# The pooling stage of a two-layer decoder step: other queues, other engines and other PSUM banks for its parts

## The reference, cut to what matters

```
cs = concat([zeros, cumsum(x_ext, axis=1)])
for g, w in enumerate((2, 4, 8, 16)):            # 256 channels each
    lo   = max(i + 1 - w, 0);  cnt = i + 1 - lo
    mean = (cs[i + 1] - cs[lo]) / cnt            # mean of the last w tokens
    d_g  = mean - x
out = einsum('btgc,gce->btge', d, w_pool) * pool_scale
x   = layernorm(ALPHA * x + out)
```

## Time and profile before

| | |
|---|---|
| median of 3 runs | 2095.04 us (2094.93 to 2096.57) |
| the profiled execution's own time | 2099.22 us |
| its span, first to last instruction | 2097.4 us |
| granted TensorE clock, mean | 0.965 |
| PE busy | 1963.5 us (94%) |
| DVE, ACT, POOL busy | 839.8, 589.9, 500.9 us |

### The profile page before, as it was taken

One profiled execution on the slowest core, in us unless ns is written; L12 is line 12 of the kernel. 1 busy time (PEld: TensorE's weight loads), 2 busy tenths in 40 slices (PEclk: granted clock), 3 DMA queues, 4 the chain that ended last, 5 costly groups with the idle time before them and its releaser, 6 DMA issues.

```text
span 2097.4 us, 36040 instructions
## 1 busy us (share of the span) xinstructions
PE 1963.5 (94%) x15430; PEld 1882.6 (90%) x15430; DVE 839.8 (40%) x1133; ACT 589.9 (28%) x822; POOL 500.9 (24%) x439
## 2 busy tenths in 40 slices
PE   7999999999988769999999999999996599999996
PEld 7999999987955558999999999999996499999996
DVE  3333322446867315333332253333225553333223
ACT  3122221333244414322122151212125352121123
POOL 3211112241310525211112131111112631111120
PEclk9999999999989879999999999999998799999998
DMA  6443222361100222223322323332221223323321
GB/s 201 145 151 100 82 89 96 87 151 41 44 1 1 84 78 81 81 81 99 90 85 91 96 81 85 95 95 85 91 91 39 62 69 92 98 82 95 97 71 41
DMA packets 260094, 179.59 MB, mean 86 GB/s; under 512 B 10870, under 2 KB 257022, under 8 KB 259485
## 3 DMA queue, kind: packets, MB, share of 16 engines
q1 hardware_dynamic: 250000, 154.90, 25.3%
q10 hardware_dynamic: 7893, 10.83, 1.9%
q0 software_dynamic: 2112, 12.59, 1.7%
HBM read 169.62 MB, written 8.08 MB: 85 GB/s over the span
## 4 chain that ended last, share of the span: by engine, by line
PE 84%; issue 6%; DVE 4%; POOL 3%; ACT 2%; DMA 1%; ACTq 0%; POOLq 0%; DVEq 0%
PE ps L845 72%; PE ps L866 3%; PE ps L972 3%; PE ps L915 2%; PE ps L977 1%; DVE w_lo L1336 1%; ACT w_hi L539 1%; PE ps L956 1%; POOL sum_sq L1873 1%; PE ps L1051 1%; POOL k_sel L1939 1%; POOL sum_z L1871 1%; PE ps L1220 1%; POOL diag L1951 1%; PE ps L994 0%
## 5 line engine op out<-in xcount | busy, mean ns | idle before, releaser
L845 PE MATMUL ps<-xh,w_hi 128*128 128x260 f32 x2880 | 592.2, 284 | 21.1 <-DVE w_lo L1336 17.4
L1336 DVE TENSOR_TENSOR w_lo<-w_raw,w_hi 128x2048 fp32r<-128x2048 f32 (+2 forms) x153 | 445.8, 2914 | 392.2 <-ACT w_hi L539 392.2
L845 PE MATMUL ps<-xh,w_lo 128*128 128x260 f32 x2880 | 589.0, 283 | 0.0
L845 PEld LDWEIGHTS ps<-xh,w_hi 128*128 128x128 f32 x2880 | 453.1, 190 | 22.8 <-DVE w_lo L1336 12.1
L845 PEld LDWEIGHTS ps<-xh,w_lo 128*128 128x128 f32 x2880 | 453.2, 190 | 0.1
L845 PE MATMUL ps<-xl,w_hi 128*128 128x260 f32 x2880 | 362.7, 283 | 0.0
L539 ACT CAST w_hi<-w_raw 128x2048 fp32r<-128x2048 f32 (+2 forms) x153 | 282.0, 1844 | 271.1 <-PE ps L845 264.0
L845 PEld LDWEIGHTS ps<-xl,w_hi 128*128 128x128 f32 x2880 | 352.9, 189 | 0.0
L845 PE MATMUL ps<-hh,w_hi 128*128 128x260 f32 x1408 | 292.9, 283 | 0.0
L845 PE MATMUL ps<-hh,w_lo 128*128 128x260 f32 x1408 | 291.4, 282 | 0.0
L1802 DVE TENSOR_TENSOR hid<-silu_g,ps 128x520 f32<-128x520 f32 x88 | 61.3, 696 | 553.6 <-ACT silu_g L755 531.7
(11 more groups left out here) (257 smaller groups left out, 1670.2 us busy)
## 6 DMA issues: line engine op xcount, KB each, us to landing
w_raw<-in_ffn_wi_dram SPq DMA_DIRECT2D x176, 512.0 KB
w_raw<-in_ffn_wo_dram SPq DMA_DIRECT2D x32, 1024.0 KB
w_raw<-in_ffn_wo_dram SPq DMA_DIRECT2D x16, 768.0 KB
w_raw<-in_attn_w_in_dram SPq DMA_DIRECT2D x8, 1024.0 KB
keys_scratch<-key_half POOLq DMA_DIRECT2D x2, 2048.0 KB, 7.9
w_raw<-in_attn_w_o_dram SPq DMA_DIRECT2D x4, 1024.0 KB
x_in<-in_x_prompt_dram ACTq DMA_DIRECT2D x4, 512.0 KB, 10.0
out_dram<-y_out ACTq DMA_DIRECT2D x4, 512.0 KB
```

What stands on the lines that cost most here:

```text
L845: mm = nc.tensor.matmul(ps[0:mc, bank + 2 * m + h, 0:HT], w[:, k, m, 0:mc], x(k)[:, h * HT:(h + 1) * HT], start=first and k == 0 and w is ...
L1336: nc.vector.tensor_tensor(w_lo[:, c % 2, 0:n], w_raw[:, c % 2, 0:n], w_hi[:, c % 2, 0:n].bitcast(F32), ALU.subtract).then_inc(s_lo, 1)
```

## The change

Everything concerns the pooling stage and its neighbours:

- **Weights**: one chunk of 1 MB for all four groups; the stage has 1 chunk where it had 4. The `f2` tail now splits this chunk and the first chunk of `f3`.
- **Values once**: `affine` writes `xf` alone. The first window addition reads `xf` and writes `win[1]`; GpSimd copies column 0.
- **State**: GpSimd issues both state transfers once `f2`'s last product is done. ACT evicts the transposed state (`state_columns`) between the two halves of the `f2` tail, ahead of `root(st, 1)`.
- **Last rows**: prompt and decode rows in one set of 8 transposes (were 16), two evictions (were four), in `last_rows`, behind the rounding of group 1.
- **Group 3's windows** remain with GpSimd and start with its own first addition of `xf`.
- **Order**: DVE makes `pooled(g)` and then `mixed(g - 1)`, the residual addition of the group before, as four instructions of 260 columns. All groups use banks 0, 2, 4, 6, so a group's products wait for the residual additions of the group before.
- **Means**: `sums` is gone in this stage. `tile_stats` multiplies each tile of x and of its square by the matrix of 1/1024 into banks 1, 3, 5, 7, between the groups' products; 32 matmuls where there were 24. ACT's squares wait for `s_sqd`, which TensorE raises per tile.

The diff, cut to its core:

```diff
@@ -512,11 +518,10 @@
     def poolmix(name):
         st = plan[name]
-        for g in range(4):
-            c = st.chunk + g
-            sp.wait_ge(s_lo, c + 1)
-            sp.dma_start(w_raw[:, c % 2, 0:512].rearrange("p (k c) -> p k c", k=2),
-                         a["pool_w"][0, g].rearrange("(k p) c -> p k c", p=P)).then_inc(s_raw[c % 2], 32)
+        c = st.chunk
+        sp.wait_ge(s_lo, c + 1)
+        sp.dma_start(w_raw[:, c % 2, :].rearrange("p (k c) -> p k c", k=KD),
+                     a["pool_w"][0].rearrange("g (k p) c -> p (g k) c", p=P)).then_inc(s_raw[c % 2], 32)
     for name in plan:
         if name == "pr":
...
@@ -555,23 +563,14 @@
         act.wait_ge(s_rv, 2 * st.ln + h + 1)
         nc.scalar.activation(moment(1, h), moment(1, h), ACT.Sqrt).then_inc(s_rstd, 1)
-    def affine(n, st, h, split, order, windows, begin, end):
+    def affine(n, st, h, split, order, begin, end):
         for at_ in range(begin, end):
             d = order[at_]
             act.wait_ge(s_t, 2 * KD * st.ln + KD * h + at_ + 1)
-            if windows:
-                if h == 0 and at_ == 0:
-                    act.wait_ge(s_wpad, 1)
-                t0, t1 = (0, HT) if h == 0 else (HT, SEQ)
-                nc.scalar.activation(win[0][:, d, 16 + t0:16 + t1], xf[:, d, t0:t1], ACT.Identity, bias=offset(n, d),
-                                     scale=gain(n, d)).then_inc(s_win, 1)
-            elif split:
+            if split:
                 nc.scalar.activation(xh[:, d, cols(h)], xf[:, d, cols(h)], ACT.Identity, bias=offset(n, d),
                                      scale=gain(n, d)).then_inc(s_xh, 1)
-            if windows and h == 1:
-                nc.scalar.activation(xf[:, d, HT:SEQ], xf[:, d, HT:SEQ], ACT.Identity, bias=offset(n, d), scale=gain(n, d))
-            t = slice(SEQ, TOK) if windows and h == 1 else cols(h)
-            nc.scalar.activation(xf[:, d, t], xf[:, d, t], ACT.Identity, bias=offset(n, d),
+            nc.scalar.activation(xf[:, d, cols(h)], xf[:, d, cols(h)], ACT.Identity, bias=offset(n, d),
                                  scale=gain(n, d)).then_inc(s_xf, 1)
     def warm(func):
...
@@ -704,23 +706,24 @@
         root(st, 0)
         if nxt is not None:
             split_hi(nxt + 1)
-        ahead = 0 if windows else 2
-        affine(n, st, 0, split, order, windows, 0, ahead)
+        ahead = 2 if between is None else 0
+        affine(n, st, 0, split, order, 0, ahead)
         for d in range(KD - 2, KD):
             act.wait_ge(s_free, first_free + d + 1)
             nc.scalar.activation(sq[:, d % 2, cols(1)], xf[:, d, cols(1)], ACT.Square).then_inc(s_sq, 1)
-        affine(n, st, 0, split, order, windows, ahead, ahead + 3)
+        affine(n, st, 0, split, order, ahead, ahead + 3)
         moments(st, 1)
-        affine(n, st, 0, split, order, windows, ahead + 3, KD)
+        affine(n, st, 0, split, order, ahead + 3, KD)
+        if between is not None:
+            between()
         root(st, 1)
-        affine(n, st, 1, split, order, windows, 0, KD)
+        affine(n, st, 1, split, order, 0, KD)
     def mixer_out(name, n, nxt):
         st = plan[name]
         for g in range(4):
-            if g > 0 or name == "op":
-                split_hi(st.chunk + g + 1, 0, 512 if name == "pl" and g < 3 else CHUNK)
+            split_hi(st.chunk + g + 1)
             if g < 3:
                 squares(st, 4 + 2 * st.group, g)
         tail(n, st, 4 + 2 * st.group, nxt, True)
...
@@ -728,27 +731,33 @@
     def poolmix(name):
         st = plan[name]
-        act.dma_start(state_in[:], a["state_pool"].rearrange("l b r d -> (l b r) d")).then_inc(s_st_in, 16)
-        act.dma_start(outs[9][:, :, 0:PBUF - 1, :].rearrange("l b r d -> (l b) r d"),
-                      a["state_pool"][:, :, 1:PBUF, :].rearrange("l b r d -> (l b) r d")).then_inc(s_tailo, 16)
+        for g in range(4):
+            for d in (2 * g, 2 * g + 1):
+                act.wait_ge(s_diff, d + 1)
+                nc.scalar.activation(xh[:, d, :], diff[:, d, :], ACT.Copy).then_inc(s_xh, 1)
+            if g == 1:
+                last_rows()
+            if g >= 1:
+                squares(st, 4 + 2 * st.group, g - 1)
+        tail(4, st, 4 + 2 * st.group, plan["f3"].chunk, True)
+    def state_columns():
         for q in range(2):
             act.wait_ge(s_st, q + 1)
             nc.scalar.activation(state_t[:, 4 * q:4 * q + 4].rearrange("p d b r -> p d (b r)"),
                                  ps[:, 6 * q, :].rearrange("p (d n) -> p d n", d=4)[:, :, 0:DEC * PBUF],
                                  ACT.Copy).then_inc(s_ste, 1)
+    def last_rows():
         act.wait_ge(s_tail, 1)
-        for n, rows in enumerate((PBUF, DEC)):
-            for q in range(2):
-                nc.scalar.activation(tail_rows[0:rows, n, q * 512:(q + 1) * 512], ps[0:rows, 2 + 2 * n + q, :],
-                                     ACT.Copy).then_inc(s_taile, 1)
-        act.wait_ge(s_taile, 4)
-        act.dma_start(outs[5].rearrange("l b r d -> (l b r) d"), tail_rows[0:PBUF, 0, :]).then_inc(s_tailo, 16)
-        act.dma_start(outs[9][0, :, PBUF - 1, :], tail_rows[0:DEC, 1, :]).then_inc(s_tailo, 16)
-        for d in range(KD):
-            act.wait_ge(s_diff, d + 1)
-            nc.scalar.activation(xh[:, d, :], diff[:, d, :], ACT.Copy).then_inc(s_xh, 1)
-        mixer_out(name, 4, plan["f3"].chunk)
+        for q in range(2):
+            nc.scalar.activation(tail_rows[:, q * 512:(q + 1) * 512], ps[0:PBUF + DEC, 3 + 4 * q, :],
+                                 ACT.Copy).then_inc(s_taile, 1)
+        act.wait_ge(s_taile, 2)
+        act.dma_start(outs[5].rearrange("l b r d -> (l b r) d"), tail_rows[0:PBUF, :]).then_inc(s_tailo, 16)
+        act.dma_start(outs[9][0, :, PBUF - 1, :], tail_rows[PBUF:PBUF + DEC, :]).then_inc(s_tailo, 16)
     def gates(st, j, off):
         act.wait_ge(s_used, off + (2 + st.chunk + j + 1))
...
@@ -1265,16 +1268,69 @@
                                          state_in[:, (4 * q + d) * P:(4 * q + d + 1) * P],
                                          ident[0:DEC * PBUF, 0:DEC * PBUF])
             mm.then_inc(s_st, 1)
-        for n, (t0, rows) in enumerate(((SEQ - PBUF, PBUF), (SEQ, DEC))):
-            for q in range(2):
-                pe.wait_ge(s_xf, st.t)
-                for d in range(4):
-                    mm = nc.tensor.transpose(ps[0:rows, 2 + 2 * n + q, d * P:(d + 1) * P],
-                                             xf[:, 4 * q + d, t0:t0 + rows], ident)
+        for q in range(2):
+            pe.wait_ge(s_xf, st.t)
+            for d in range(4):
+                mm = nc.tensor.transpose(ps[0:PBUF + DEC, 3 + 4 * q, d * P:(d + 1) * P],
+                                         xf[:, 4 * q + d, SEQ - PBUF:TOK], ident)
         mm.then_inc(s_tail, 1)
-        pe.wait_ge(s_taile, 4)
         pe.wait_ge(s_ste, 2)
-        return mixer_out(name)
+        pe.wait_ge(s_lo, st.chunk + 3)
+        for g in range(3):
+            group_products(st, g, (0, 1)).then_inc(s_group, 1)
+            if g == 1:
+                pe.wait_ge(s_taile, 2)
+            if g >= 1:
+                tile_stats(st, 2 * g - 2, (0, 1))
+                tile_stats(st, 2 * g - 1, (0, 1))
+        group_products(st, 3, (0,)).then_inc(s_first, 1)
+        group_products(st, 3, (1,)).then_inc(s_used, 1)
+        for d in (4, 5):
+            tile_stats(st, d, (0, 1))
+        for d in (6, 7):
+            mm = tile_stats(st, d, (0,))
+        mm.then_inc(s_stat, 1)
+        def left():
+            for d in (6, 7):
+                mm = tile_stats(st, d, (1,))
+            mm.then_inc(s_stat, 1)
+        return left
+    def group_products(st, g, only):
+        c = st.chunk
+        wh = w_hi[:, c % 2, :].rearrange("p (g k u c) -> p g k u c", g=4, k=2, u=2)[:, g]
+        wl = w_lo[:, c % 2, :].rearrange("p (g k u c) -> p g k u c", g=4, k=2, u=2)[:, g]
+        if g >= 1 and 0 in only:
+            pe.wait_ge(s_free, 4 + 2 * st.group + 2 * g)
+        for x, s_ready, ws in ((xh, s_xh, (wh, wl)), (xl, s_x, (wh,))):
+            for k in range(2):
+                pe.wait_ge(s_ready, st.x + 2 * g + k + 1)
+                for m in range(2):
+                    for w in ws:
+                        for h in only:
+                            mm = nc.tensor.matmul(ps[:, 4 * m + 2 * h, 0:HT], w[:, k, m, :], x[:, 2 * g + k, cols(h)],
+                                                  start=k == 0 and w is wh and x is xh, stop=k == 1 and x is xl)
+        return mm
+    def tile_stats(st, d, of):
+        first_free = 4 + 2 * st.group
+        for q in range(2):
+            for h in of:
+                if q == 0:
+                    if d >= 6 and h == 0:
+                        pe.wait_ge(s_last, 2 * st.ln + d - 5)
+                    else:
+                        pe.wait_ge(s_free, first_free + d + 1)
+                else:
+                    pe.wait_ge(s_sq, SQUARES * st.ln + (d + 1 if d < 6 else d + 1 + 2 * h))
```

(55 more changed lines are left out.)

72 lines of the change are left out of this document (31 added, 41 removed).

## The result

Before 2095.44 us (2094.93 to 2096.57), after 2078.86 us (2077.75 to 2083.26), the medians of four executions each; the ratio is 0.9916, 95% interval 0.9899 to 0.9932. That is 16.6 us less, where 21.4 were forecast. The profiled execution of the changed kernel took 2083.26 us with a span of 2081.4: it is the slowest of its four, and 2.02 us of it lie ahead of everything that was changed (`f2`'s last product ends at 1605.54 here and at 1603.5 before). Times of this profile are therefore compared with forecast ones after taking off 2.02.

What follows compares the result with a forecast made beforehand. TensorE was taken to bound the kernel except in the pooling stage, where completion of the first half's means sets the end. 19.6 us there plus 1.8 in `f3` make 21.4: 2095.04 to 2073.6 us, range 2068.5 to 2081.5.

Steps and rivals of the forecast that it cites:

- The path: Pooling stage: completion of the first half's means, 1676.11 before, sets the end; each us earlier is a us of the kernel.
- Part 1: Up to group 0's differences: second root 1614.5, last value 1620.2, differences 1627.1 instead of 1630.64; gain there 3.5 us.
- Part 2: State load from GpSimd's queue: issued at 1603.6, landing before 1611.5, in time for the second root; price nothing.
- late-state rival: State lands at 1614.9, with 3.35 us for an issue held by VectorE's split; 3.4 us lost, 2077.0; chance 0.11.
- the rule that it cites: Trainium skill: GpSimd's descriptor writing is shut out while a VectorE instruction uses both ports; some 3 us worse if it applies.
- Part 3, VectorE's chain: Groups 1 to 3, VectorE alternating with GpSimd: differences at 1633.5, 1642.1 and 1646.9, `mixed(1)` done at 1643.7.
- Part 3, TensorE from there: From 1643.7, products of groups 2 and 3 and means at 0.22 us each at full clock: first-half means complete at 1656.5.
- this sign of being wrong: Profile sign in the stage: mean matmuls dearer than 0.22 us at the full clock and 0.40 at the low one.
- Part 3, the clock: Group 2's products: low clock after TensorE idles 3 to 4 us, taking 5.3 us, to 1649.0.
- Part 3, the weights: One chunk split in `f2`'s tail, three splits inside the stage gone: no gain beyond the timetable, no loss.
- Part 4: Inside `f3`: four mean matmuls for the second half remain of twelve, 0.88 us instead of 2.63; 1.8 us gained.
- The sum: Whole kernel: 19.6 us from earlier first-half means plus 1.8 inside `f3`, 21.4 us together; profiled execution 2077.8, median 2073.6.

Runs made afterwards that it cites:

- e7: Changed kernel with each value written twice again by ScalarE, also into `win[0]`, which nothing reads, decode tokens apart in the second half: 2080.67 us.
- e4: Changed kernel with both state transfers issued by ScalarE instead of GpSimd, behind the first root of `f2`'s tail: 2078.75 us.
- e5: Changed kernel with GpSimd issuing the state transfers later, behind its wait for the first half's values of `xf`: 2081.74 us.
- e6: Changed kernel without the means of x for tiles 2 to 5, eight mean matmuls fewer: 2074.29 us.
- e1: Changed kernel with group 3's second-half products and second-half means of tiles 4 and 5 moved behind the first half's last mean: 2075.19 us.
- e10: Changed kernel with the squares and their mean matrix rounded, so their 16 mean matmuls take rounded operands: 2076.36 us.
- e8: Changed kernel with pooling weights in four pieces of 256 KB, splits of pieces 2 to 4 and `f3`'s first chunk inside the stage: 2084.64 us.
- e3: Changed kernel with GpSimd summing x and its squares again for tiles 0 to 5, group by group behind its `xl`: 2087.86 us.
- e2: e1 plus second-half means of tiles 2 and 3 moved there too, with four buffers for the squares, not two: 2073.09 us.
- a0: The changed kernel run again unchanged, as control: 2077.79 us.
- e9: e2 plus GpSimd's third and fourth window additions of group 3 held until VectorE finished group 1's and group 2's differences: 2073.37 us.

## Why the prediction was right or wrong

**The path, and that the change would shorten it: right.** It was said that the moment of the first half's means sets the end and each us of it is a us of the kernel; the 371.5 to 371.6 us behind the stage in all thirteen profiles show it.

**Part 1: right.** By the other profile's time, second root 1614.56 (forecast 1614.5), last value 1620.7 (1620.2), group 0's differences 1627.44 (1627.1). e7 prices the single write in the new order at 2.6 us.

**Part 2: right in its price of nothing; its ground for a worse case isn't borne out.** The state landed at 1610.5 by the other profile's time, an us before 1611.5. e4 shows time to spare, e5 that the price starts at one for one when it is used up. The 3.35 us that the late-state rival added, for an issue held by VectorE's split, don't show: in e5 both issues stood within such a split and took 0.59 and 0.56 us. The prediction applied the rule that it cites to that split; the measurement shows that the split doesn't hold the issue of a direct transfer. Why the indirect one took 2.92 us, the runs leave open.

**Part 3, VectorE's chain: right.** Taking turns with GpSimd gave group differences at 1633.8, 1642.4 and 1647.2 (forecast 1633.5, 1642.1, 1646.9), `mixed(1)` at 1644.1 (1643.7).

**Part 3, TensorE from there: the mis-sized step.** "A mean matmul costs 2.63/12 = 0.22 at the full clock ... eight of them 1.75." The eight of tiles 2 and 3 took 3.51, and twelve (tiles 4 and 5, and the first half of 6 and 7) 5.27. The same slip is in the counts: the 24 of the kernel before, set against the 32 of the new one, are records of 12 matmuls; 32 matmuls are 64 records. The forecast's own rows held the answer, six matmuls to a half in the code and x12 in the earlier trace rows. From the residual additions' end to the means' end 12.8 us were forecast and 14.8 measured: group 2's products 3.16 for 5.3 (-2.1), the means behind them +1.7, group 3's products -0.3, the last means 5.27 for 2.5 (+2.8). With the 0.4 by which VectorE came late that is the 2.4 by which 1658.9 misses 1656.5. One slip is inside the sum itself: four matmuls of 0.22 are 0.88, and the forecast took 0.7 for them and the squares. e6 shows the 0.44, e1 its place in the queue. The prediction had named this sign of being wrong, mean matmuls dearer than 0.22, and it is the one that came.

**Part 3, the clock: wrong, on the other side.** Group 2's products were taken at the low clock because TensorE would have been idle 3 to 4 us. With matmuls of twice the length the means of tiles 0 and 1 filled half of that pause: 1.74 us, and the clock stayed full. One slip made both errors, and they offset each other in part: with means of 0.44 and the low clock that was forecast, the means would have been complete at 1660.9, as an estimate (1643.7 + 5.3 + 3.51 + 3.1 + 5.27), and not at 1658.9. That the forecast missed by 3.4 us and not by some 5 is luck. e10 (3.01 us), e8 (4.28) and e3 (8.01) have the low clock in this place.

**Part 3, the weights: no price where there is one.** "No gain beyond the timetable, no loss": e8 takes 5.6 us for splits in my places inside the stage, 2.4 of them VectorE's delay and the rest the low clock that follows. For the forecast this changes nothing, since its timetable had no splits in it; as an account of what the change is worth it is incomplete. In the kernel before, TensorE's 10.67 us of waiting for `w_lo` lay beside the chain, which ran through GpSimd's sums.

**Part 4: half.** `f3` keeps 8 mean records in place of 12, 1.75 us for 2.63, so 0.88 saved and not 1.8; B is 0.83 shorter.

**The sum.** 17.2 + 0.8 = 18.0 in place of 19.6 + 1.8 = 21.4. The profiled execution would then have been 2099.22 - 18.0 = 2081.2, and 2083.26 is that and the 2.02 ahead of the stage. Each undone alone in the changed kernel, the means cost 8.5 us and the weights 5.6, both in the order tried, the single write 2.6, the queue of the state nothing. Such prices need not add up to 18.0; the shared banks and the joined last rows weren't tried alone.

## What to carry to other kernels

Before a duration per instruction is taken from a grouped row, count in the code how many instructions the row stands for; a row's count is of records, and in these profiles a matmul with fp32 operands is two. When the end of a stage is one engine's queue, look for what in it the next stage doesn't need yet, and whether the same engine has a pause behind: moving work there was worth more (4.7 us) than making VectorE's waits vanish (1.1 more) or rounding half of the mean matmuls (1.6). And price a clock along with a pause: less work ahead of a wait lengthens the pause, and can cost what it saved.

## What the runs showed of the hardware

- A mean matmul of 260 columns with fp32 operands leaves two records, 0.44 us together at the full clock; with rounded ones it leaves one. Six of the last twelve rounded, in e10, made 3.36 us of 5.27.
- Before group 2's products the granted clock was the full one behind pauses of 0.47 to 0.48 us (e1, e2, e7) and of 1.73 to 1.74 (the changed kernel, a0, e4, e5, e6), the low one behind 3.01, 4.28 and 8.01. The pause doesn't settle it alone. Group 1's products stayed at the full clock (two in 0.40) behind 1.77 us in the changed kernel; behind the same 1.77 in e9 and behind 1.88 in e2 they began at the full clock and fell to the low one (0.64) after some 1.5 us. Nor does it settle how long the low clock lasts: behind the same 6.04 us `f3`'s first 18 product records took 3.93 us in the changed kernel and 4.24 in e7, e8 and e10. Why, in either case, the runs leave open.
- 480 KB landed in 6.7 us (6.3 in a0) from GpSimd's queue, issued 0.13 us behind SyncE's loads of `f3`'s weights; in 4.88 from the same queue 7 us later; and in 4.8 from ScalarE's, issued 0.15 us ahead of those loads. Whether the queue or the place among the loads makes the difference wasn't told apart.
- A split on VectorE with two inputs in SBUF held GpSimd's copy (1.39 us in place of 0.24) and not its issues of direct transfers (0.59 and 0.56 us inside the split, e5).
- Of a loosened wait, little arrives. Of 3.6 us won at group 0 in e9, 1.1 came out at the end: 0.8 went where group 2's additions met GpSimd, 1.7 where VectorE waited for GpSimd's last window addition and then worked beside its `xl`.
